# Reordering VectorE around LayerNorm, splitting two more weights, and summing one modulation slice on GpSimd

## The reference

```python
for l in range(2):
    mod = silu(c) @ ada_w[l] + ada_b[l]            # 1024 x 6144 weights
    shift1, scale1, gate1, shift2, scale2, gate2 = split(mod, 6)
    h = rms_norm(x, norm1_g[l]) * (1 + scale1) + shift1
    z = h @ w_in[l]                                # q, k, v, ga, gb, gates
    o = diff_attention(rope(q), rope(k), v, lam)   # softmax minus lam * softmax
    o = rms_norm(o, subln_g[l]) * (1 - lambda_init)
    u = causal_depthwise_conv(ga * sigmoid(gb), w, bias)   # 31 taps, 512 channels
    u = silu(layer_norm(u, conv_ln_g[l], conv_ln_b[l]))
    g_attn, g_conv = split(sigmoid(z[gates]))
    mixed = (g_attn * (o @ w_attn_o[l]) + g_conv * (u @ w_conv_o[l])) @ w_out[l]
    x = x + (1 + gate1) * mixed
    h2 = rms_norm(x, norm2_g[l]) * (1 + scale2) + shift2
    x = x + (1 + gate2) * swiglu(h2, w_ffn_in[l], w_ffn_out[l])
x = rms_norm(x, final_g)
```

## Time and profile before

| | |
|---|---|
| median of 3 runs | 2461.19 us |
| the profiled execution | 2462.88 us, span 2460.6 us |
| TensorE busy | 2392.4 us, 97% |
| VectorE busy | 1936.9 us, 79% |
| ScalarE busy | 1409.5 us, 57% |
| GpSimd busy | 17.4 us, 1% |
| mean granted TensorE clock | 0.994 |
| DMA | 653 MB, mean 265 GB/s |

### The profile page before, as it was taken

One profiled execution on the slowest core, in us unless ns is written; L12 is line 12 of the kernel. 1 busy time (PEld: TensorE's weight loads), 2 busy tenths in 40 slices (PEclk: granted clock), 3 DMA queues, 4 the chain that ended last, 5 costly groups with the idle time before them and its releaser, 6 DMA issues.

```text
span 2460.6 us, 31549 instructions
## 1 busy us (share of the span) xinstructions
PE 2392.4 (97%) x12767; PEld 2053.1 (83%) x12767; DVE 1936.9 (79%) x1864; ACT 1409.5 (57%) x1402; POOL 17.4 (1%) x33
## 2 busy tenths in 40 slices
PE   5999999999999999999999999999999999999998
PEld 5987888989888899898888988888888888888886
DVE  6997878788797665775445769898989898989897
ACT  2653433645533454464344557777777777777776
POOL 0000000000000000000000000000000000000000
PEclk9999999999999999999999999999999999999999
DMA  9556989444598445455555449999999999999996
GB/s 345 190 179 240 316 303 345 148 137 158 191 350 279 153 151 180 151 178 183 185 186 180 163 143 365 354 364 348 362 354 357 354 365 348 362 355 361 349 365 219
DMA packets 434775, 653.03 MB, mean 265 GB/s; under 512 B 20145, under 2 KB 323889, under 8 KB 434625
## 3 DMA queue, kind: packets, MB, share of 16 engines
q1 hardware_dynamic: 432592, 644.63, 76.4%
q0 software_dynamic: 2032, 6.33, 0.8%
HBM read 649.82 MB, written 1.05 MB: 265 GB/s over the span
## 4 chain that ended last, share of the span: by engine, by line
PE 89%; DVE 7%; ACT 2%; issue 1%; DMA 1%; SPq 0%; ACTq 0%; DVEq 0%
PE pair L2016 27%; PE pair L2018 26%; PE pair L2017 26%; PE pair L2048 3%; PE tb L2223 2%; DVE rest L1140 2%; PE pair L2405 1%; DVE aw L1509 1%; PE pair L2137 1%; PE tb L2097 1%; DMA raw<-in_ada_w 1%; DVE gat L1159 1%; ACT aw L720 1%; DVE hT L1259 1%; PE pair L2151 0%
## 5 line engine op out<-in xcount | busy, mean ns | idle before, releaser
L1140 DVE TENSOR_TENSOR rest<-raw,head 128x2048 fp32r<-128x2048 f32 x542 | 1240.2, 2291 | 289.6 <-ACT head L691 273.7
L691 ACT ACTIVATE head<-raw 128x2048 fp32r<-128x2048 f32 x542 | 1035.6, 1912 | 320.7 <-PE pair L2018 283.9
L2016 PE MATMUL pair<-head,hTh 128*128 128x512 f32 x1664 | 665.4, 400 | 6.5 <-DVE hTl L1214 2.9
L2018 PE MATMUL pair<-head,hTl 128*128 128x512 f32 x1664 | 650.7, 391 | 0.0
L2017 PE MATMUL pair<-rest,hTh 128*128 128x512 f32 x1664 | 649.4, 390 | 0.0
L2016 PEld LDWEIGHTS pair<-head,hTh 128*128 128x128 f32 x1664 | 312.9, 188 | 72.9 <-issue 5.4
L2018 PEld LDWEIGHTS pair<-head,hTl 128*128 128x128 f32 x1664 | 312.7, 188 | 66.4
L2017 PEld LDWEIGHTS pair<-rest,hTh 128*128 128x128 f32 x1664 | 313.4, 188 | 61.8 <-issue 1.2
L2016 PE MATMUL pair<-hTh,head 128*128 128x256 f32 x1104 | 314.6, 285 | 6.3 <-issue 2.3
L2018 PE MATMUL pair<-hTh,rest 128*128 128x256 f32 x1104 | 312.4, 283 | 0.0
L2017 PE MATMUL pair<-hTl,head 128*128 128x256 f32 x1104 | 312.3, 283 | 0.0
(11 more groups left out here) (307 smaller groups left out, 1798.7 us busy)
## 6 DMA issues: line engine op xcount, KB each, us to landing
raw<-in_moe_w_gate SPq DMA_DIRECT2D x224, 512.0 KB, 5.3
raw<-in_moe_w_up SPq DMA_DIRECT2D x224, 512.0 KB, 7.1
raw<-in_moe_w_down SPq DMA_DIRECT2D x224, 512.0 KB, 5.9
raw<-in_w_in SPq DMA_DIRECT2D x152, 512.0 KB, 4.6
raw<-in_ada_w SPq DMA_DIRECT2D x96, 512.0 KB, 5.6
raw<-in_w_ffn_in SPq DMA_DIRECT2D x88, 512.0 KB, 5.7
raw<-in_w_ffn_out SPq DMA_DIRECT2D x44, 512.0 KB, 5.4
raw<-in_w_out SPq DMA_DIRECT2D x40, 512.0 KB, 4.5
```

Source lines behind the costliest of these rows:

```text
L691: act.activation(head[:, c.split, :], raw[:, c.raw, :], ACT.Copy).then_inc(heads_done, 1)
L1140: dve.tensor_tensor(rest[:, c.split, :], raw[:, c.raw, :], head[:, c.split, :].bitcast(F32), ALU.subtract).then_inc(rests_done, 1)
L2016: pe.matmul(out_, lh, rh, start=start, stop=False, skip_group_check=True)
L2018: return pe.matmul(out_, ll, rh, start=False, stop=stop, skip_group_check=True)
```

## The change

Six edits, all in the first block's mixers:

- The modulation chunks of (0,4) come before those of (0,2) and are loaded sooner: one each before gates0.3, yattn0.0, yattn0.1 and yconv0.0. Those of (0,2) follow before yconv0.1 and before three of the four chunks of wout0.
- GpSimd accumulates (0,4): 15 instructions of 128 x 1024, each waiting for the one before, from the end of the attention product (`pv0`). It multiplies in place in `raw` and adds. Load n+6 after such a chunk waits for GpSimd's `pool_freed`. TensorE sums (0,4) before wout0.0 instead of inside wout0.1, and VectorE takes it before the first half's add.
- The two chunks of `yconv0` are split like the others.
- `channel_stats` becomes `channel_mean`, placed behind one rest instead of two, and `channel_scale`, placed behind the second.
- In the second mixer, taps 11 and 12 go before the masks, taps 16 and 17 between the rests of gates1.2, and tap 22 before `head_scale`.

```diff
-            queue_mods((0, 3), (0, 2), (0, 4))
+            queue_mods((0, 3), (0, 4), (0, 2))
...
         plan.split(f"attn{l}.0")
+        plan_mods(1 if l == 0 else 0)
         plan_linear(f"gates{l}.3", w, NT, "act", 2560 + 3 * NT)
         plan.split(f"attn{l}.1")
         plan.job(f"lnturn{l}", "act")
+        plan_mods(1 if l == 0 else 0)
         plan_linear(f"yattn{l}.0", a["w_attn_o"][l], NT, "dve", rows=KW)
...
-            plan_linear(f"yconv{l}.{j}", a["w_conv_o"][l], NT, "dve", j * NT, rows=KW, unsplit=l == 0)
+            plan_linear(f"yconv{l}.{j}", a["w_conv_o"][l], NT, "dve", j * NT, rows=KW)
...
-                plan_mods((2 if (j, ch) == (0, 0) else 1) if l == 0 else 0)
+                plan_mods(1 if l == 0 and (j, ch) != (1, 1) else 0)
...
+                elif n - RAW in POOLED:
+                    load(n, POOLED.index(n - RAW) + 1, landed[n % RAW], parts, freed=sem("pool_freed"))
...
+            def modulation_sum(k, j):
+
+                acc = accumulator(SLICES.index((k, j)))
+                pool.wait_ge(job_done, jobs_done("pv0"))
+                for i, n in enumerate(POOLED):
+                    pool.wait_ge(landed[n % RAW], 32 * (n // RAW + 1))
+                    for h in range(2):
+                        src, c_ = raw[:, n % RAW, h * D:(h + 1) * D], cact[:, 2 * i + h:2 * i + h + 1]
+                        if i == 0 and h == 0:
+                            own.did(pool.tensor_scalar(acc, src, c_, None, ALU.mult))
+                        else:
+                            own.did(pool.tensor_scalar(src, src, c_, None, ALU.mult))
+                            own.now()
+                            own.did(pool.tensor_tensor(acc, acc, src, ALU.add))
+                        own.now()
+                    pool.sem_inc(sem("pool_freed"), 1)
+                pool.sem_inc(sem("pool_sum_ready"), 1)
...
-                if q == 0 and i >= 2:
+                if q == 0 and i >= 2 and (k, j) != (0, 2):
                     dve.wait_ge(sem("mod_summed"), mod_part(*SLICES[i - 1]))
...
+                if l == 1:
+                    conv_taps(l, range(11, 13))
                 mask_and_max(l, 0)
                 mask_and_max(l, 1)
-                conv_taps(l, range(11, 16))
+                conv_taps(l, range(11 if l == 0 else 13, 16))
...
+                if l == 1:
+                    feed(last_chunk("gates1.2"))
+                    conv_taps(l, range(16, 18))
                 feed(last_chunk(f"gates{l}.2") + 1)
-                conv_taps(l, range(16, 22))
+                conv_taps(l, range(16, 22) if l == 0 else range(18, 23))
                 head_scale(l)
-                conv_taps(l, range(22, 24))
+                conv_taps(l, range(22 if l == 0 else 23, 24))
...
-                feed(last_chunk(f"gates{l}.3") + 1 + AHEAD)
-                channel_stats(l)
+                feed(last_chunk(f"yattn{l}.0") + 1)
+                channel_mean(l)
+                feed(last_chunk(f"yattn{l}.1") + 1)
+                channel_scale(l)
...
-                                taken=(((0, 2, 0), (0, 2, 1)), ((0, 4),)) if l == 0 else ((), ()))
+                                taken=(((0, 4), (0, 2, 0), (0, 2, 1)), ()) if l == 0 else ((), ()))
...
             def mix(k):
+                if k == 0:
+                    mod_sum(0, 4)
                 linear(f"wout{k}.0", NT, busy=8 if k == 0 else 0, splits=(f"mix{k}.0", f"mix{k}.1"))
                 for part in ((0, 2, 0), (0, 2, 1)) if k == 0 else ():
                     mod_sum(*part)
-                linear_by_tiles(f"wout{k}.1", (1, 3, 5)[k], x if k < 2 else xn, sums=((0, 4),) if k == 0 else ())
+                linear_by_tiles(f"wout{k}.1", (1, 3, 5)[k], x if k < 2 else xn)
```

More of the change, by code:

```diff
@@ L317, in build @@
     UNSPLIT = sorted(plan.unsplit)
+    POOLED = [n for n, entry in enumerate(plan.seq) if entry[0] == "m" and SLICES[entry[1][0]] == (0, 4)]
     def split_chunks(k):
@@ L323, in freed_by_rests @@
     def freed_by_rests(n):
-        return n + 1 - sum(1 for m in UNSPLIT if PLACE[m] <= n)
+        return n + 1 - sum(1 for m in UNSPLIT if PLACE[m] <= n) - sum(1 for m in POOLED if m <= n)
     STEPS3 = F3 // FB
@@ L647, in gate_bias @@
                 pool.dma_start(gbc[:, j // 3, :], src[:, j * D:(j + 1) * D].to_broadcast([P, D])).then_inc(sem(f"gate_bias{k}_{j}"), 16)
+            def modulation_sum(k, j):
[14 more added lines that the diff above has]
+                pool.sem_inc(sem("pool_sum_ready"), 1)
             gate_bias(0, 2)
             gate_bias(0, 5)
+            modulation_sum(0, 4)
             pool.wait_ge(evac["dve"], plan.jobs["norm1.1"][4])
@@ L1171, in mods_now @@
                 while seen[0] < len(plan.seq) and plan.seq[seen[0]][0] == "m":
-                    mod_chunk(seen[0])
+                    if seen[0] not in POOLED:
+                        mod_chunk(seen[0])
                     seen[0] += 1
@@ L1525, in head_scale, with channel_mean, channel_scale @@
                                   over(orms, [P, 8, P], 2), ALU.mult).then_inc(evac["dve"], 1)
-            def channel_stats(l):
+            def channel_mean(l):
                 dve.wait_ge(sem("ln_sums"), l + 1)
                 dve.tensor_scalar(lnsum, lnsum, -1.0 / W, None, ALU.mult).then_inc(sem("ln_mean"), 1)
+            def channel_scale(l):
                 dve.wait_ge(sem("ln_root"), l + 1)
@@ L2087, in mod_sum @@
             def mod_sum(k, j, part=0):
-                pe.wait_ge(sem("acc_ready"), SLICES.index((k, j)) + 1)
+                if (k, j) == (0, 4):
+                    pe.wait_ge(sem("pool_sum_ready"), 1)
+                else:
+                    at = SLICES.index((k, j))
+                    pe.wait_ge(sem("acc_ready"), at + 1 - (at > SLICES.index((0, 4))))
                 acc = accumulator(SLICES.index((k, j)))
```

## The result

The changed kernel takes 2468.31 us (median of 9 runs), the kernel before beside it 2461.84 (9 runs): ratio 1.0026, 95% interval 1.0017 to 1.0035, slower by 6.5 us. The prediction said 2451. The profiled execution took 2468.82 us with a span of 2466.8; its first mixer begins at 146.87 instead of 145.84 because the first loads landed later (ScalarE's wait for `x` ends at 18.54 us instead of 17.74), before anything that was changed.

What follows compares the result with a forecast made beforehand. TensorE holds 89% of the chain, so VectorE's work shows only where TensorE waits, in each mixer's tail. Gains of 8.9 us (first mixer) and 1.5 (second), 10.4 together, take the 2461.19 median to 2451; range 2446 to 2473.

Steps and rivals of the forecast that it cites:

- GpSimd's own work: First mixer, from the attention product's end: 8 multiplies and 7 adds take 20.8 us, ready before 180.
- second estimate of 2.25: GpSimd's add priced from the Trainium skill's 4497 ns for 2048: 2.25 us each, total 23 us.
- bound of 3.6 us each: GpSimd's operations in the first mixer: up to 3.6 us each, the sum is in time and SP's queue costs nothing.
- first rival: Taps and rests, 146 to 172: GpSimd's operations hold VectorE up one for one, up to 20.8 us, 2472; chance 0.25 in full.
- norm transposes: End of the first mixer: the transposes that start at 238.13 were to start at 229.25.
- first mixer, gain: First mixer up to the norm transposes: 8.9 us sooner, handed on by the feed-forward.
- second mixer, gain: Second mixer, moved taps and the mean 2.8 us sooner: 1.5 us gained, bounds 0.6 and 2.8.
- LayerNorm's order: First mixer: mean 4 us sooner, of which 2.0 reach the path; convolution product starts 2.7 us sooner.
- The 2.2 of the split weights: First mixer's convolution product: 13.98 us becomes 11.75, 2.2 less, for two more VectorE rests of 2.29 us.
- Second rival: GpSimd late, above 3.6 us per operation: TensorE and SP's queue wait, 2461.6; chance 0.11 together with an even trade.
- The third: First mixer: VectorE wasn't what ended last, gain only 2.2 and 2.0, 2456; chance 0.12 together with partial hold-up.
- rule quoted against the change: VectorE instructions with two SBUF inputs and GpSimd ones reading SBUF exclude each other for a whole instruction; would give the first rival's sum.

Runs made afterwards that it cites:

- e12: Changed kernel without GpSimd's part, all modulation on VectorE, slice (0,4) still summed before (0,2); 2454.49 us, ratio 0.9969 to the kernel before.
- e2: Changed kernel with fourteen of GpSimd's fifteen multiplies and adds left out, (0,4) not computed; 2452.43 us, ratio 0.9958 to the kernel before.
- e1: Kernel before with every edit but GpSimd's part, slice (0,4) on VectorE in its old places; 2455.30 us, ratio 0.9973 to the kernel before.
- e7: Kernel before with only LayerNorm's mean and scale issued between the feeds, in both mixers; 2457.37 us, ratio 0.9983 to the kernel before.
- e9: Changed kernel with GpSimd starting only at the end of the taps, some 26 us later; 2477.31 us, ratio 1.0061 to the kernel before.
- e3: Changed kernel with GpSimd's seven adds left out, its eight multiplies kept; 2456.27 us, ratio 0.9977 to the kernel before.
- e5: Separate kernel of 16 phases, nothing of the model: GpSimd and VectorE operations alone and side by side; adds beside taps 18.10 us, alone 9.33 and 9.65.
- e10: Changed kernel with one GpSimd multiply, buffers released at once, seven adds behind the taps, (0,4) not computed; 2455.68 us, ratio 0.9971 to the kernel before.

## Why the prediction was wrong

The step that failed is *GpSimd's own work*, whose term in the sum was nothing: "20.8, ready before 180", "hidden". In its place the runs show 19.33 us of the first mixer, taken from VectorE while its taps were what TensorE waited for. Two things were wrong in the step, and the second is the one that decided.

- **Its length.** The multiply was taken as the memset's 0.94 us and takes 2.83 alone; the add as 1.9 and takes 2.31, near the second estimate of 2.25. In the kernel all fifteen are busy 46.3 us, 3.1 each. A memset has no tensor to read; its row was the nearest by engine and shape, not by kind. This alone would have cost nothing by the prediction's own bound of 3.6 us each.
- **Its cover.** It was taken to run beside VectorE at no cost. It doesn't, as the first rival said (chance 0.25): place (the taps), direction and start condition were right. Its price was "up to the whole 20.8", "one for one", decisive from 10.4; measured are 19.33, and not one for one but out of 46.3 us of operations. That the figure is near is luck: too short a length was multiplied by too full an exclusion. Each add among the taps holds them for 2.16 us, each multiply for 0.63.

The trade in one line: on VectorE slice (0,4) costs 4.44 us of the first mixer (e12 minus e2; 6.23 from e1, whose sums stand in the old order), on GpSimd 19.33 (after minus e2). A fused multiply-add of 1.28 us was replaced by an add that holds VectorE for longer than that, and a multiply on top.

The rest of the sum stood. With GpSimd nearly idle (e2), times from the start of the stretch:

| step | forecast | e2 |
|---|---|---|
| mean issued | 28.8 | 28.52 |
| output product, second half | 66.2 | 65.03 |
| norm transposes | 83.4 | 82.75 |
| first mixer, gain | 8.9 | 9.55 |
| second mixer, gain | 1.5 | 1.94 after, 1.99 in e1 |
| time | 2451 | 2452.4 |

Inside the 8.9 the terms overlap, and that their sum came out within 0.7 is partly luck. LayerNorm's order is worth 2.20 alone; the convolution product starts 3.7 us sooner (188.30, e7), not 2.7, but 1.5 of it is lost again by the end, since VectorE is packed. The 2.2 of the split weights are 0.46 alone and 1.12 behind LayerNorm's order (100.35 to 99.23). Most comes from the slice's leaving and the order of the sums that goes with it (4.44 and 1.79), which make room for the rests that the split needs. One reading in the prediction was wrong without consequence: between the two rests ahead of the mean at 178.56 stands a whole modulation chunk (0.75 and 1.29 us at 174.37 and 175.16), not half of one.

Second rival, GpSimd late: the sum is ready 48.2 us behind the start of the stretch and TensorE reaches it at 73.3, so it was not late here. In e2, without the delay, TensorE reaches it at 54.0, which would still have been in time; e9 shows its mechanism in SP's queue, at 26 us later. The third falls: VectorE was what ended last, as the 4.44 show. The Trainium skill's rule quoted against the change (SBUF — State Buffer, Who interferes with whom) was the right one to fear: with the adds the runs agree, nearly whole instructions exclude each other (18.10 of 18.98). With the multiply they don't for the whole instruction: it reads SBUF too, yet 24 taps and four of them take 12.80 us, not the sum of 21.05. It can itself be held whole, as by the two rests in e3 (6.99 us). That copies and multiplies on VectorE are held as well (14.90, 13.58) fits the same section of the Trainium skill, by which they can take the shared pair in a mode that uses two ports; whether they ran in that mode no run shows. The lack of any effect with an input in PSUM and with the memset agrees with it.

## What to carry to other kernels

Work given to GpSimd is not free when VectorE is full: before moving an elementwise operation there, count how long it holds VectorE and compare that with what it costs on VectorE itself. Here that is about 2.2 us for an add of 128x1024 and 0.6 to 0.8 for the multiply before it, against 1.28 for the fused one, a loss where VectorE works from SBUF without slack. Put GpSimd's adds, if at all, beside VectorE operations that read PSUM (no effect in e5) or beside its idle time (0.5 us each in e10, where both stand), and release loading buffers independently of them. And price an operation from a row of its own kind: one small kernel (e5) shows the multiply's 2.83 us, and the 18.10 of adds and taps side by side.

## What the runs showed of the hardware that was not expected

- GpSimd's one-input multiply (2.83 us for 128x1024) is slower than its two-input add (2.31), and its copy takes 1.0.
- A GpSimd multiply holds VectorE for a part of its length: one tap of 128x256 for 0.8 us, but two of VectorE's own one-input multiplies for 0.9 and 0.8 us (1.20 and 1.11 us where the others take 0.34). So 24 of these go from 6.39 to 12.90 us beside GpSimd multiplies, and 24 taps from 9.59 to 12.73.
- The holding goes both ways: a GpSimd add lasted 6.32 us and a multiply 6.99 us behind two rests of VectorE.
- Cutting an add into four doesn't help: 17.16 us for the phase against 18.10, and the adds' own time grows from 9.78 to 13.66.
- Operations of 128x2 are held by adds as the large ones are: 24 of them go from 3.29 to 12.05 us beside four adds.
